# Where the last output-projection unit is split, and which expert loads take the freed places

## The chip, the cores and the metric

The kernel runs on one core of a Trainium2 chip. The core has a matrix engine (TensorE, PE in the profile), a vector engine (VectorE, DVE), a scalar engine (ScalarE, ACT), GpSimd (POOL) and SyncE (SP), which here issues nearly all DMA transfers. They work from an on-chip memory, SBUF, and matrix products land in the banks of PSUM. Engines wait for one another through semaphores. The metric is the time of one execution in microseconds.

## The reference

Two transformer blocks run one after the other on 256 tokens of 1024 channels. The first is a gated mix of three branches and a feed-forward part. The second has two kinds of attention, an output projection, and a mixture of 32 experts, of which each token uses two:

```python
mixed = concat(rmsnorm(o_dil), rmsnorm(o_sb))
x = x + gate_mix * (mixed @ w_out)
h2 = modulate(rmsnorm(x, g_ffn), shift_ffn, scale_ffn)
y = hierarchical_moe(h2, w_group, w_expert, w_gate, w_up, w_down)
x = x + gate_ffn * y
return rmsnorm(x, g_final)
```

The change lies between `mixed @ w_out` and the first expert. The norm ahead of the experts needs the sum of squares of every token over its 1024 channels, and the routing needs the product of `x` with `w_group` and `w_expert` (36 columns, the logits), scaled by that norm.

## The kernel before

**Units.** All weights but those of the experts come as a stream of units of 1 MiB. A unit lands in a raw buffer. ScalarE copies each half of it, rounded, to a high part (`sph`, line 1314), and GpSimd subtracts that from the raw data and writes the low part (`spl`, line 2596). TensorE then makes three products for each pair of operands (lines 538 to 540). High and low part of a unit together fill one of `NSP` = 3 split places, `u.n % NSP`. ScalarE may write a half of a unit only when TensorE has used the unit three before it (`half_used`, line 1313). The output projection is the last stage of the stream, with the four units `w_out_units` 0 to 3. Units 0 and 3 therefore share a split place, and units 1 and 2 have the two others.

**TensorE's order around the change.** `out_part(n, ks, ...)` multiplies unit n, in two halves of 128 output channels each. After the attention it runs: unit 0 (its last 12 matmuls in each half), unit 1, unit 2, then `logits(0)` to `logits(3)`, then the whole of unit 3 (48 matmuls), then `logits(4)` to `logits(6)`, the first matmuls of the sums of squares (line 1114), `logits(7)`, and the last matmuls of the sums (line 1118). The transposes of line 1127 follow. `logits(k)` (line 1096, 4 matmuls) waits for channel block k of the new `x`, `XTN[:, k]`.

**VectorE.** For k = 0 to 7 it makes `XTN[:, k]` out of PSUM (line 2353), as soon as half k of the eight halves is used. From k = 2 on it first waits for the square k - 1 and adds it to the running sum `SQA` (line 2350). Behind these come the reciprocal root and the routing, from line 2363.

**ScalarE.** After the attention's last parts it takes the splits of the remaining units, the last of which is unit 3, and then makes the eight squares (line 1774), in program order. The root of the sums is line 1776.

**Expert loads.** The weights of the 32 experts (6 MiB each) come as half loads of 1 MiB, numbered 0, 1, 2, ... in `EXPERT_WEIGHTS`; from 34 on most are taken in pairs of 2 MiB. Each goes to a place in a ring of SBUF regions. The early loads go to regions that other data leaves free one after the other, and the list `ISSUED` gives the order in which SyncE issues them. SyncE waits before each for what frees its place, and everything behind it in the list waits too. Loads 15 to 22 go to what the output projection frees: 15 and 16 to `ring5`, 17 and 18 to `ring6`, 19 and 20 to `ring7` (the split places of the units 1, 2 and 3 by `TOP_OF`), 21 and 22 to `ring8` (the projection's left operand). Load 14 goes to the raw buffer of the last unit, once that is split. Loads from 24 on wait until an expert has used the earlier load in their place; load 24 waits for the first quarter of expert 0.

Of the kernel before, what the change touches and what calls it, by code (L numbers as in the profile page):

```python
# [22 lines left out]
NSP = 3  # L23
# [78 lines left out]
def k8(t):  # L102
    return t.rearrange("p (k n) -> p k n", k=8)
# [119 lines left out]
def program(nc, I, out, const_at):  # L223
    with ExitStack() as ctx:
# [43 lines left out]
            return v if k is None else v.rearrange("p (k n) -> p k n", k=k)  # L268

        units, first, ada_at, ff_at, wide_at, conv_at = stream_plan()  # L270


        G = ar(0, 6144).rearrange("p (i t n) -> p i t n", i=3, t=2)
# [52 lines left out]
        w_out_units = [units[first["w_out_2"] + n] for n in range(4)]  # L326
        RING = [at(f"ring{n}", TOP - 4096 - 4096 * n, 4096) for n in range(2)]
        RING += [at("ring2", O_RAW, 4096), at("ring3", O_XB, 4096), at("ring4", O_RAW + 4096, 4096)]
        TOP_OF = {n + 4: O_SPL + 4096 * (w_out_units[n].n % NSP) for n in (1, 2, 3)}
        for n in (5, 6, 7):  # L330
            RING.append(at(f"ring{n}", TOP_OF[n], 4096))
        RING += [at("ring8", O_XA, 4096), at("ring9", O_AR + 10496, 4096)]
# [5 lines left out]
        SLOT += [ar(6144, 2048), ar(8192, 2048)]  # L338

        FIRST = [0, 1, 2, NS, 3, 4, 5, NS + 1, 6, 7, 8, 9, NS - 2] + list(range(10, NS - 2)) + [NS - 1]  # L340
        ISSUED = [0, 1, 2, 4, 8, 12, 5, 6, 9, 10, 11, 3, 7, 13, 15, 16, 14] + list(range(17, 23)) + list(range(24, 34))
        ISSUED += [23] + list(range(34, len(EXPERT_WEIGHTS)))

        def place(s):
# [158 lines left out]
        def tensor(e):  # L503
# [42 lines left out]
            def fm_unit(v, name, xT, ready):  # L546

                u = units[v]
                H, L = k8(SPH[u.n % NSP]), k8(SPLO[u.n % NSP])
                b = bank(name)  # L550
                claim(b)
                for h in range(2):
                    c = slice(h * 128, h * 128 + 128)
                    w.wait_ge(lo_ok, 2 * u.n + h + 1)
                    for k in range(8):
                        if ready:
                            w.wait_ge(*ready(k))
                        mm = product(ps[b][:, h * 256:h * 256 + 256], H[:, k, c], L[:, k, c], xT[0][:, k, :],
                                     xT[1][:, k, :], k == 0, k == 7)
                    mm.then_inc(w.up(half_used), 1)  # L560
                return b

            def tm_part(stage, n, outs, xT, ready, tiles, done):

                u, i = units[unit_at(stage, n)], n % 2
                H, L = k4(SPH[u.n % NSP]), k4(SPLO[u.n % NSP])
                for h in range(2):
                    w.wait_ge(lo_ok, 2 * u.n + h + 1)
                    for tt in tiles:
                        c = slice(tt * 128, tt * 128 + 128)  # L570
                        for k in (2 * h, 2 * h + 1):
                            if ready:
                                w.wait_ge(*ready(4 * i + k, tt))
                            mm = product(outs[tt], xT[0][:, 4 * i + k, c], xT[1][:, 4 * i + k, c], H[:, k, :], L[:, k, :],
                                         i == 0 and k == 0, i == 1 and k == 3)
                        if tt == 0 and i == 1 and h == 1:
                            mm.then_inc(w.up(tile0_mm), 1)
                    if done:
                        mm.then_inc(w.up(half_used), 1)
# [37 lines left out]
            def wide(v, bb, xT, start, stop, tiles=(0, 1)):  # L617

                u = units[v]
                H, L = k2(SPH[u.n % NSP]), k2(SPLO[u.n % NSP])  # L620
                for k in range(2):
                    w.wait_ge(lo_ok, 2 * u.n + k + 1)
                    for j in range(2 * tiles[0], 2 * tiles[-1] + 2):
                        cc, cn = slice((j // 2) * 128, (j // 2) * 128 + 128), slice((j % 2) * 512, (j % 2) * 512 + 512)
                        claim(bb[j])
                        mm = product(ps[bb[j]][:, :], xT[0][:, k, cc], xT[1][:, k, cc], H[:, k, cn], L[:, k, cn],
                                     start and k == 0, stop and k == 1)
                        if stop and k == 1 and j < 3:
                            mm.then_inc(w.up(wide_mm), 1)
                    if 1 in tiles:  # L630
                        mm.then_inc(w.up(half_used), 1)
# [379 lines left out]
            def out_part(n, ks, start, stop, halves=(0, 1)):  # L1011

                u = units[first["w_out_2"] + n]
                H, L = k8(SPH[u.n % NSP]), k8(SPLO[u.n % NSP])
                for h in halves:
                    if start:
                        b = bank(("w_out_2", 2 * n + h))
                        claim(b)
                        held.add(b)
                    b = bank_of["w_out_2", 2 * n + h]  # L1020
                    c = slice(h * 128, h * 128 + 128)
                    w.wait_ge(lo_ok, 2 * u.n + h + 1)
                    for k in ks:
                        w.wait_ge(act_lo, part_at["heads_s" if k >= 4 else "heads_d"] + k % 4 // 2 + 1)
                        mm = product(ps[b][:, 0:256], H[:, k, c], L[:, k, c], XA[0][:, k, :], XA[1][:, k, :],
                                     start and k == ks[0], stop and k == ks[-1])
                    if stop:
                        mm.then_inc(w.up(half_used), 1)
                        free[b] = [(x_ok, X4 + 2 * n + h + 1)]
# [72 lines left out]
                logits(k)  # L1102
            release(0)
            out_part(3, range(8), True, True)
            for k in range(4, 7):
                logits(k)
            for n in (1, 2, 3):
                release(n)
            b = bank("ss")
# [2 lines left out]
            w.wait_ge(sqa_ok, 6)  # L1112
            for tt in range(2):
                e.matmul(ps[b][:, tt:tt + 1], SQA[:, tt * 128:tt * 128 + 128], ones[:, 0:1], start=(tt == 0), stop=False)
            logits(7).then_inc(w.up(rt_mm), 1)
            w.wait_ge(hs_ok, 8)
            for tt in range(2):
                mm = e.matmul(ps[b][:, tt:tt + 1], SQ2[1][:, tt * 128:tt * 128 + 128], ones[:, 0:1], start=False, stop=(tt == 1))
            mm.then_inc(w.up(ss_mm), 1)
            free[b] = [(rs_ok, 1)]  # L1120
            for i in range(4):
                tt, half = i % 2, i // 2
# [171 lines left out]
        def scalar(e):  # L1294
# [9 lines left out]
            def split_one(between=None):  # L1304
# [4 lines left out]
                for h in range(2):  # L1309
                    if h and between:  # L1310
                        between()
                    if u.n >= NSP:
                        w.wait_ge(half_used, 2 * (u.n - NSP) + (h + 1 if u.same else 2))
                    e.activation(u.half(SPH[u.n % NSP], h), u.half(RAW[u.slot], h), ACTF.Copy).then_inc(w.up(hi_ok), 1)  # L1314

            def take(v):

# [1268 lines left out]
        def gpsimd(e):  # L2586
# [3 lines left out]
            def split_one():  # L2590
# [2 lines left out]
                begun[0] += 1  # L2593
                for h in range(2):
                    w.wait_ge(hi_ok, 2 * u.n + h + 1)
                    e.tensor_tensor(u.half(SPLO[u.n % NSP], h), u.half(RAW[u.slot], h), u.half(SPH[u.n % NSP], h),  # L2596
                                    ALU.subtract).then_inc(w.up(lo_ok), 1)

            split_one()
# [7 lines left out]
        def sync(e):  # L2607
# [38 lines left out]
            for n, s in enumerate(ISSUED):  # L2646
# [25 lines left out]
                elif s in (6, 7, 11):  # L2672
                    pass
                elif 15 <= s < 23:
                    w.wait_ge(half_used, 2 * w_out_units[min((s - 13) // 2, 3)].n + 2)
                elif s == 23:
                    w.wait_ge(y0_mm, 1)
                else:
# [180 lines left out]
```

## Time and profile before

| | us |
|---|---|
| median of 3 runs | 1093.62 |
| lowest and highest | 1093.51, 1094.03 |
| profiled execution, time | 1094.04 |
| profiled execution, span of the trace | 1092.3 |
| TensorE busy | 996.4 |
| VectorE, ScalarE, GpSimd busy | 529.8, 391.5, 498.3 |
| mean DMA rate over the span | 313 GB/s |

The profile has a page (busy time of the engines, 40 slices of the span, the chain of work that ended last) and a trace that can be asked for windows, for the instructions of an engine in order of time, and for the DMA issues with their time to landing. Times in the trace count from the start of the span. A row of a timeline gives start, duration, engine, line, operation, tiles and shapes, how many instructions are merged into it, and in brackets how long the engine had been idle and what ended that.

### The profile page before, as it was taken

How to read it: one execution, taken by the hardware profiler on the slowest of the kernel's cores; microseconds unless marked ns; L12 is line 12 of the kernel's file. 1: busy time of each engine (PE TensorE's matmuls, PEld its weight loads, DVE VectorE, ACT ScalarE, POOL GpSimd, SP SyncE). 2: the span in 40 equal slices, each digit the busy share in tenths (PEclk: the TensorE clock that was granted, in tenths of full speed). 3: DMA queues.
4: the chain of work that ended last, by engine and by line, in shares of the span. 5: the costliest groups of instructions: out<-in, count | busy, mean ns of one | idle time of the engine just before them, and what ended most of it. 6: DMA issues, size and time to landing. Idle time of an engine off the chain costs nothing.

```text
span 1092.3 us, 16613 instructions
## 1 busy us (share of the span) xinstructions
PE 996.4 (91%) x6890; PEld 733.6 (67%) x6890; DVE 529.8 (49%) x984; ACT 391.5 (36%) x558; POOL 498.3 (46%) x210
## 2 busy tenths in 40 slices
PE   7999999999999999999899999999968687878786
PEld 6989988788788888887898895544434343434332
DVE  1998896665367776214358543323222121222224
ACT  7345555554475444556597441000000000000002
POOL 6987699879598887987666510000000000000000
PEclk9999999999999999999899999999999899999888
DMA  9745455547469999638343989999999999999995
GB/s 381 280 168 180 153 194 193 182 186 278 154 248 397 356 360 377 245 116 338 131 155 116 367 347 417 429 424 428 424 428 426 426 428 425 427 427 426 427 422 239
DMA packets 38527, 341.96 MB, mean 313 GB/s; under 512 B 4273, under 2 KB 4657, under 8 KB 6322
## 3 DMA queue, kind: packets, MB, share of 16 engines
q1 hardware_dynamic: 37152, 337.82, 77.2%
q10 hardware_dynamic: 1298, 3.05, 0.8%
q8 instruction: 55, 0.90, 0.3%
q14 instruction: 22, 0.18, 0.0%
HBM read 339.81 MB, written 1.05 MB: 312 GB/s over the span
## 4 chain that ended last, share of the span: by engine, by line
PE 63%; DMA 24%; DVE 6%; ACT 3%; SPq 1%; issue 1%; POOL 0%; another core or an unknown queue 0%; DVEq 0%; ACTq 0%
DMA ring<-in_gu 17%; PE ps L538 15%; PE ps L540 15%; PE ps L539 15%; DMA ring<-in_dn 7%; PE ps L1187 5%; PE ps L1229 4%; PE ps L1218 2%; PE ps L1168 1%; SPq L2680 1%; PE ps L720 1%; ACT sph L1314 1%; DVE ar L2294 1%; SPq L2654 0%; PE ps L1206 0%
## 5 line engine op out<-in xcount | busy, mean ns | idle before, releaser
L2596 POOL TENSOR_TENSOR spl<-raw,sph 128x1024 fp32r<-128x1024 f32 x204 | 496.3, 2467 | 139.9 <-ACT sph L1314 139.8
L1314 ACT ACTIVATE sph<-raw 128x1024 fp32r<-128x1024 f32 x204 | 208.4, 1056 | 107.6 <-PE ps L540 93.3
L2604 POOL TENSOR_SCALAR ring<-ring,SM 128x512 f32<-128x512 f32 x1 | 1.6, 1567 | 449.9 <-DVE SM L1854 449.9
L1806 ACT ACTIVATE ar<-ps 64x256 f32<-64x256 f32 x32 | 12.1, 377 | 331.8 <-PE ps L1187 331.8
L538 PE MATMUL ps<-sph,xbh 128*128 128x512 f32 x304 | 119.6, 394 | 0.4 <-DVE ar L2261 0.4
L540 PE MATMUL ps<-sph,xbl 128*128 128x512 f32 x304 | 118.5, 390 | 0.0
L539 PE MATMUL ps<-spl,xbh 128*128 128x512 f32 x304 | 118.4, 389 | 0.0
L1229 PE MATMUL ps<-ar,ar 128*128 128x512 f32 x240 | 111.9, 609 | 0.0
L538 PE MATMUL ps<-xah,sph 128*128 128x256 f32 x320 | 92.1, 288 | 1.1 <-DVE xal L1869 0.8
L1899 DVE SCALAR_TENSOR_TENSOR ps<-ar,COL,ps 128x256 f32<-128x256 f32 x232 | 92.1, 480 | 0.0
L539 PE MATMUL ps<-xal,sph 128*128 128x256 f32 x320 | 90.5, 283 | 0.0
L540 PE MATMUL ps<-xah,spl 128*128 128x256 f32 x320 | 90.5, 283 | 0.0
L1187 PE MATMUL ps<-ring,ar 128*32 128x256 f32 x944 | 63.7, 413 | 25.9 <-DMA ring<-in_gu 25.9
L2538 DVE TENSOR_TENSOR ar<-ar,ps 64x256 f32<-64x256 f32 x32 | 13.5, 423 | 141.3 <-ACT ar L1806 141.3
L1229 PEld LDWEIGHTS ps<-ar,ar 128*128 128x128 f32 x240 | 45.6, 201 | 47.6 <-issue 47.6
L538 PE MATMUL ps<-sph,xah 128*128 128x512 f32 x192 | 75.7, 394 | 1.5 <-POOL spl L2596 1.5
L539 PE MATMUL ps<-spl,xah 128*128 128x512 f32 x192 | 74.8, 389 | 0.0
L540 PE MATMUL ps<-sph,xal 128*128 128x512 f32 x192 | 74.8, 389 | 0.0
L1187 PEld LDWEIGHTS ps<-ring,ar 128*32 128x32 f32 x944 | 31.2, 115 | 63.2 <-issue 47.9
L1187 PE MATMUL ps<-ring,xg 128*32 128x256 f32 x912 | 58.6, 398 | 15.3 <-DMA ring<-in_gu 14.7
L1218 PE MATMUL ps<-ring,ar 128*32 128x512 f32 x464 | 55.9, 595 | 17.3 <-DMA ring<-in_dn 16.1
L538 PEld LDWEIGHTS ps<-sph,xbh 128*128 128x128 f32 x304 | 57.1, 188 | 12.3 <-DVE ar L2261 0.8
(332 smaller groups left out, 1708.2 us busy)
## 6 DMA issues: line engine op xcount, KB each, us to landing
raw<-in_stream SPq DMA_DIRECT2D x127, 1024.0 KB, 5.8
ring<-in_gu SPq DMA_DIRECT2D x46, 2048.0 KB, 45.6
ring<-in_dn SPq DMA_DIRECT2D x22, 2048.0 KB, 45.7
ring<-in_gu SPq DMA_DIRECT2D x24, 1024.0 KB, 9.5
ring<-in_dn SPq DMA_DIRECT2D x14, 1024.0 KB, 10.9
ar<-in_gu SPq DMA_DIRECT2D x7, 1024.0 KB, 30.7
slotx<-in_gu SPq DMA_DIRECT2D x5, 1024.0 KB, 43.8
ar<-in_dn SPq DMA_DIRECT2D x3, 1024.0 KB, 47.8
```

The source lines that it names most:

```text
L538: e.matmul(o, sh, mh, start=start, stop=False)
L539: e.matmul(o, sh, ml, start=False, stop=False)
L540: return e.matmul(o, sl, mh, start=False, stop=stop)
L720: mm = e.matmul(ps[b][:, d * 256:d * 256 + 256], WP[:, g, k, d * 128:d * 128 + 128], ZP[:, 2 * g + k, 16:272], start=(k == 0), stop=(k == 1))
L1187: mm = e.matmul(ps[b][32 * q:32 * q + 32, 0:256], XG[g % 2][:, k, (x % 4) * 32:(x % 4) * 32 + 32], W[:, q // 2, k % 2, (q % 2) * 256:(q % ...
L1218: mm = e.matmul(ps[b][32 * j:32 * j + 32, :], HE[x % 2][:, 32 * j:32 * j + 32], W[:, 2 * (j % 2) + j // 2, :], start=True, stop=True)
L1229: mm = e.matmul(ps[yb[tt * 2 + nn]][:, :], SWT[x % 2][:, tt * 128:tt * 128 + 128], YP[x % 2][:, nn * 512:nn * 512 + 512], start=False, sto ...
L1314: e.activation(u.half(SPH[u.n % NSP], h), u.half(RAW[u.slot], h), ACTF.Copy).then_inc(w.up(hi_ok), 1)
L1806: e.activation(HS[x % 2][0:64, :], ps[bank_of["gu", x]][0:64, 0:256], ACTF.Silu).then_inc(w.up(hsa_ok), 1)
L1899: e.scalar_tensor_tensor(out=acc if k < 30 else CVO[:, c, :], in0=CV[:, c, k:k + 256], scalar=tap(k, c), in1=acc, op0=ALU.mult, op1=ALU.add)\
L2538: e.tensor_tensor(h[0:64, :], h[0:64, :], ps[bank_of["gu", x]][64:128, 0:256], ALU.mult).then_inc(w.up(hsm_ok), 1)
L2596: e.tensor_tensor(u.half(SPLO[u.n % NSP], h), u.half(RAW[u.slot], h), u.half(SPH[u.n % NSP], h), ALU.subtract).then_inc(w.up(lo_ok), 1)
```

## The change

Unit 3 is split into the place of unit 1 in place of that of unit 0 (`split_at`), so ScalarE waits for the halves of unit 1 before it writes them. The split place of unit 0 becomes `ring5`, and that of unit 1, now also unit 3's, becomes `ring7`. So loads 15 and 16 wait for unit 0, 17 and 18 for unit 2, and 19 to 22 for unit 3. Load 14 is issued behind 17 and 18. On TensorE, the first matmuls of the sums of squares come straight behind unit 3, then `logits(4)` and `logits(5)`, then the last matmuls of the sums, then `logits(6)` and `logits(7)`.

```diff
+        last_unit = units[first["w_out_2"] + 3]
+
+        def split_at(u):
+
+            return (u.n + 1 if u is last_unit else u.n) % NSP
...
-        TOP_OF = {n + 4: O_SPL + 4096 * (w_out_units[n].n % NSP) for n in (1, 2, 3)}
+        TOP_OF = {ring: O_SPL + 4096 * split_at(w_out_units[n]) for ring, n in ((5, 0), (6, 2), (7, 3))}
...
-        ISSUED = [0, 1, 2, 4, 8, 12, 5, 6, 9, 10, 11, 3, 7, 13, 15, 16, 14] + list(range(17, 23)) + list(range(24, 34))
+        ISSUED = [0, 1, 2, 4, 8, 12, 5, 6, 9, 10, 11, 3, 7, 13, 15, 16, 17, 18, 14] + list(range(19, 23)) + list(range(24, 34))
...
             release(0)
             out_part(3, range(8), True, True)
-            for k in range(4, 7):
-                logits(k)
             for n in (1, 2, 3):
                 release(n)
             b = bank("ss")
...
             w.wait_ge(sqa_ok, 6)
             for tt in range(2):
                 e.matmul(ps[b][:, tt:tt + 1], SQA[:, tt * 128:tt * 128 + 128], ones[:, 0:1], start=(tt == 0), stop=False)
-            logits(7).then_inc(w.up(rt_mm), 1)
+            for k in (4, 5):
+                logits(k)
             w.wait_ge(hs_ok, 8)
             for tt in range(2):
                 mm = e.matmul(ps[b][:, tt:tt + 1], SQ2[1][:, tt * 128:tt * 128 + 128], ones[:, 0:1], start=False, stop=(tt == 1))
             mm.then_inc(w.up(ss_mm), 1)
+            logits(6)
+            logits(7).then_inc(w.up(rt_mm), 1)
...
-                    if u.n >= NSP:
+                    if u is last_unit:
+                        w.wait_ge(half_used, 2 * w_out_units[1].n + h + 1)
+                    elif u.n >= NSP:
                         w.wait_ge(half_used, 2 * (u.n - NSP) + (h + 1 if u.same else 2))
-                    e.activation(u.half(SPH[u.n % NSP], h), u.half(RAW[u.slot], h), ACTF.Copy).then_inc(w.up(hi_ok), 1)
+                    e.activation(u.half(SPH[split_at(u)], h), u.half(RAW[u.slot], h), ACTF.Copy).then_inc(w.up(hi_ok), 1)
...
                 elif 15 <= s < 23:
-                    w.wait_ge(half_used, 2 * w_out_units[min((s - 13) // 2, 3)].n + 2)
+                    w.wait_ge(half_used, 2 * w_out_units[(0, 2, 3, 3)[(s - 15) // 2]].n + 2)
```

## Rows read from the trace of the kernel before

**Rows 1.** The page's 40 slices of the span: GB/s that the DMA engines moved.

```profile
GB/s 381 280 168 180 153 194 193 182 186 278 154 248 397 356 360 377 245 116 338 131 155 116 367 347 417 429 424 428 424 428 426 426 428 425 427 427 426 427 422 239
```

**Rows 2.** Windows: length, busy PE, PEld, DVE, ACT, POOL, PEclk, DMA share, GB/s.

```profile
633.00:636.00 3.00, 3.00 (x28) 3.00 (x27) 1.49 (x3) 1.30 (x4) 3.00 (x2) 1.00 0.00 0
637.00:1040.00 403.00, 338.19 (x3082) 176.24 (x3082) 112.85 (x266) 32.00 (x78) 0.00 (x0) 0.96 1.01 425
...
652.00:656.00 4.00, 3.89 (x34) 3.63 (x38) 1.87 (x7) 2.15 (x5) 0.00 (x0) 1.00 1.02 424
```

**Rows 3.** The chain that ended last, 1040 to 1092: its last transfer (start, us).

```profile
1048.62 31.83 DMA ring<-in_dn
```

**Rows 4.** Timeline of SyncE: issues of loads 15, 17, 19 and 24.

```profile
635.09 0.33 SPq L2680 DMA_DIRECT2D ring<-in_dn  x1
...
637.97 0.33 SPq L2680 DMA_DIRECT2D ring<-in_gu  x1
...
645.51 0.33 SPq L2680 DMA_DIRECT2D ring<-in_gu  x1
...
657.00 0.33 SPq L2680 DMA_DIRECT2D ring<-in_gu  x1
```

**Rows 5.** Issue to landing: issued 605.29 to 608.73 (min), 635.09, 645.51, 657.00.

```profile
DMA to landing us min/median/max: 5.2/6.7/7.3
...
DMA to landing us min/median/max: 5.1/5.1/5.1
...
DMA to landing us min/median/max: 8.1/8.1/8.1
...
DMA to landing us min/median/max: 6.6/6.6/6.6
```

**Rows 6.** The page's DMA issues: count, KB each, median us from issue to landing.

```profile
ring<-in_gu SPq DMA_DIRECT2D x46, 2048.0 KB, 45.6
```

**Rows 7.** Timeline of TensorE: logits 0 to 3, unit 3's first matmul, what follows.

```profile
637.77 1.87 PE L1096 MATMUL ps<-cst,xtn 128*128 128x36 f32 x16
639.48 0.36 PE L538 MATMUL ps<-xah,sph 128*128 128x256 f32 x1
...
645.32 1.43 PE L1096 MATMUL ps<-cst,xtn 128*128 128x36 f32 x12
...
647.47 0.58 PE L1118 MATMUL ps<-cst,ar 128*128 128x1 f32 x4
...
652.02 0.38 PE L1151 MATMUL ps<-AS,cst 128*128 128x32 f32 x2 [1.27 <-DVE AS L2402]
```

**Rows 8.** Timeline of VectorE: blocks of XTN (L2353), adds (L2350), first routing step.

```profile
630.78 0.48 DVE L2353 SCALAR_TENSOR_TENSOR xtn<-ps,SM,ar 128x256 f32<-128x256 f32 x1 [1.25 <-PE ps L540]
...
633.92 0.73 DVE L2350 TENSOR_TENSOR ar<-ar,ar 128x256 f32<-128x256 f32 x1 [1.22 <-ACT ar L1774]
634.76 0.48 DVE L2353 SCALAR_TENSOR_TENSOR xtn<-ps,SM,ar 128x256 f32<-128x256 f32 x1
635.73 1.48 DVE L2350 TENSOR_TENSOR ar<-ar,ar 128x256 f32<-128x256 f32 x1 [0.48 <-ACT ar L1774]
...
638.27 0.42 DVE L2350 TENSOR_TENSOR ar<-ar,ar 128x256 f32<-128x256 f32 x1 [0.48 <-ACT ar L1774]
...
648.66 0.54 DVE L2363 SCALAR_TENSOR_TENSOR RT<-ps,SM 128x36 f32<-128x36 f32 x2
```

**Rows 9.** Timeline of ScalarE: unit 3's first half, first two squares, the root.

```profile
630.83 1.06 ACT L1314 ACTIVATE sph<-raw 128x1024 fp32r<-128x1024 f32 x1 [2.27 <-PE ps L540]
...
633.18 0.70 ACT L1774 ACTIVATE ar<-xtn 128x256 f32<-128x256 f32 x2
...
648.09 0.26 ACT L1776 ACTIVATE SM<-ps,cst 128x2 f32<-128x2 f32 x1 [1.64 <-PE ps L1118]
```

**Rows 10.** Timeline of GpSimd: the two halves of the last unit.

```profile
631.97 2.40 POOL L2596 TENSOR_TENSOR spl<-raw,sph 128x1024 fp32r<-128x1024 f32 x1 [9.73 <-ACT sph L1314]
...
634.33 2.59 POOL L2596 TENSOR_TENSOR spl<-raw,sph 128x1024 fp32r<-128x1024 f32 x1
```

More of the change, by code:

```diff
@@ L548, in fm_unit @@
                 u = units[v]
-                H, L = k8(SPH[u.n % NSP]), k8(SPLO[u.n % NSP])
+                H, L = k8(SPH[split_at(u)]), k8(SPLO[split_at(u)])
                 b = bank(name)
@@ L565, in tm_part @@
                 u, i = units[unit_at(stage, n)], n % 2
-                H, L = k4(SPH[u.n % NSP]), k4(SPLO[u.n % NSP])
+                H, L = k4(SPH[split_at(u)]), k4(SPLO[split_at(u)])
                 for h in range(2):
@@ L619, in wide @@
                 u = units[v]
-                H, L = k2(SPH[u.n % NSP]), k2(SPLO[u.n % NSP])
+                H, L = k2(SPH[split_at(u)]), k2(SPLO[split_at(u)])
                 for k in range(2):
@@ L1013, in out_part @@
                 u = units[first["w_out_2"] + n]
-                H, L = k8(SPH[u.n % NSP]), k8(SPLO[u.n % NSP])
+                H, L = k8(SPH[split_at(u)]), k8(SPLO[split_at(u)])
                 for h in halves:
@@ L2595, in split_one @@
                     w.wait_ge(hi_ok, 2 * u.n + h + 1)
-                    e.tensor_tensor(u.half(SPLO[u.n % NSP], h), u.half(RAW[u.slot], h), u.half(SPH[u.n % NSP], h),
+                    e.tensor_tensor(u.half(SPLO[split_at(u)], h), u.half(RAW[u.slot], h), u.half(SPH[split_at(u)], h),
                                     ALU.subtract).then_inc(w.up(lo_ok), 1)
```

## The prediction

> **What bounds the kernel now.** I read the page's 40 slices first. In the GB/s row [rows 1] the last 14 slices before the final one stand at 422 to 429: whatever TensorE does there, the 16 DMA engines are full. The table of windows [rows 2] makes this sharp. From 637 to 1040 us the DMA share is 1.01 at 425 GB/s, so a load of 1 MiB (1.049 MB) takes 1.049/425 = 2.47 us of the stream. Just ahead of that stretch there is a hole: 633 to 636 stands at 0.00. Then the chain of what ended last [rows 3]: its late pieces are transfers, and the last expert load lands at 1048.62 + 31.83 = 1080.45, with 12 us of the last expert's work and the output behind it. So the end is the end of the load stream plus a fixed tail, and a change pays only by what it moves the stream.
>
> The stream waits for places. The issues of SyncE [rows 4] show what ends the hole: load 15 at 635.09, when the second output unit is used up. Each later issue then meets some backlog. A load issued into idle DMA engines lands after 5.1 us, and 5.2 in the other such case; the one issued at 645.51 lands after 8.1, the one at 657.00 after 6.6 [rows 5]. The excess over 5.1 is the backlog at that moment: 8.1 - 5.1 = 3.0 us and 6.6 - 5.1 = 1.5 us. **The second number decides this case**: it belongs to expert load 24, the first that has to wait for an expert to be computed (gu_mm, the first quarter of expert 0). In the median the loads of the stream land 45.6 us behind their issue [rows 6], so nothing later is as tight. If the stream is moved ahead by more than 1.5 us and the routing in front of expert 0 isn't, a new hole opens there.
>
> **Part 1: loads 15 and 16 into the first unit's place.** Times of TensorE: between 639.48 and 645.32 the last unit's 48 matmuls start, 0.12 us apart [rows 7]. A half unit of 12 is 1.44 us. VectorE takes the first half of unit 0 at 630.78 [rows 8], so the halves of units 0 and 1 end at 630.78, 632.22, 633.66 and 635.10; the last agrees with the issue at 635.09 [rows 4]. Load 15 goes out at 632.2 in place of 635.1: 2.9 us earlier. It lands at 632.2 + 5.1 = 637.3, load 16 at 639.7. Load 17 still waits for unit 2, at 637.97 [rows 4], and can't land before 637.97 + 5.1 = 643.1, while the stream alone would give 639.7 + 2.5 = 642.2: 0.9 us are lost again. So after this stop the stream is 2.9 - 0.9 = 2.0 us ahead. Moving load 14 behind 17 and 18 costs nothing: its wait (the last unit's low parts) ends before load 19 may go.
>
> **Part 2: the last unit split into the second unit's place.** ScalarE's two halves, the first at 630.83 with 1.06 us [rows 9], waited for unit 0 and began 0.06 behind its halves. Now they wait for the halves of unit 1: start 633.72, end 634.78, and start 635.16, end 636.22. TensorE doesn't feel that directly: GpSimd's first half then runs from 634.86 to 637.26 (2.40 [rows 10]), the second to about 639.8, and TensorE wants them at 639.5 and 642.4. What is queued behind the wait does. On ScalarE the eight squares of the sums stand behind the split in program order. The first two ran at 633.18 (0.70 for both [rows 9]); now they start at 636.13 and end at 636.83. VectorE may not make xtn 2 until it has added square 1 (it waits hs_ok, adds, then goes on), so that add comes at 636.86.
>
> And the adds run into GpSimd. The add L2350 takes 0.42 alone, as at 638.27 [rows 8]. The one at 633.92 took 0.73 and ended 634.65, 0.28 after GpSimd's first half ended (631.97 + 2.40 = 634.37 [rows 10]); the one at 635.73 took 1.48 and ended 637.21, again 0.28 after GpSimd's second half (634.33 + 2.59 = 636.92). So an add (two operands in SBUF) is held until the running subtraction ends, while L2353 (one operand in PSUM) took its usual 0.48 at 634.76, inside it. Now: the add at 636.86 is held to 637.26 + 0.28 = 637.54. From an add's end to the next block of xtn it is 0.10, the block takes 0.48, and from there to the next add, with a square between, it is 0.49 (635.24 to 635.73) [rows 8]. So xtn 2 runs from 637.64 to 638.12 and the next add is ready at 638.61. GpSimd's second half is running: with the 2.59 that it took before it ends at 637.22 + 2.59 = 639.81, and the add at 640.09. xtn 3 runs from 640.19 to 640.67. TensorE needs xtn 3 for logits(3), which stands ahead of the last unit in its queue. Before, xtn 3 was ready at 637.21 + 0.10 + 0.48 = 637.79, well before its turn (16 matmuls from 637.77 on, 0.11 apart, the last four from 639.05 [rows 7]). Now logits(3) starts at about 640.67 + 0.15 = 640.82 (for the release I take a little over the 0.10 that VectorE needs for its own) and the last unit 0.45 later, at 641.27 in place of 639.48. **The last unit is 1.8 us late**, and with it the places that it frees.
>
> **Part 3: sums of squares ahead of the last logits.** Before, behind the last unit came 12 logits matmuls, 4 for the sums, 4 for logits(7) and 4 for the rest of the sums, which ended at 647.47 + 0.58 = 648.05 [rows 7]; then the root at 648.09 [rows 9], a reciprocal, and L2363 at 648.66 [rows 8], 0.61 behind the sums. From 645.32 to 647.47 20 matmuls start, so one takes 0.1075. With the new order, and the last unit ending 1.8 later (647.11), the last four for the sums start 12 matmuls on, at 648.40, and end at 648.98; the root's way would let L2363 start at 649.59. But it needs logits(6) and logits(7) too, which now stand last: the 24th matmul starts at 647.11 + 23 x 0.1075 = 649.58 and ends 0.28 later, and L2363 comes at about 649.95. Against 648.66 that is 1.3 late: of the 1.8 the new order gives 0.5 back. Without the delay, part 3 would be worth that 0.5 and no more, since 24 matmuls have to run in either order.
>
> **The sum.** Load 19 goes out at 645.51 + 1.8 = 647.3 and lands at 652.4 (the stream alone would give 650.4); four loads end at 652.4 + 3 x 2.47 = 659.8 against 661.0 before: 1.2 ahead. Load 24 goes out at 657.00 + 1.3 = 658.3 and lands at 658.3 + 5.1 = 663.4 against 657.00 + 6.6 = 663.6: **0.2 us ahead**. In general the gain is the least of 2.0, 3.0 - d and 1.5 - (d - 0.5), with d the delay of the last unit; for d = 1.8 the three are 2.0, 1.2 and 0.2. Later issues have more backlog than that and the stream is full to 1080, so this is what reaches the end. The profiled execution has a span of 1092.3 and a time of 1094.04; changed, it would have 1092.1 and 1093.8. It lies 0.42 above the median of the runs, so against the median the forecast is 1093.62 - 0.2 = 1093.4. The landing into idle engines (5.1 or 5.2 [rows 5]) moves it by 0.1, the release of logits(3) (nothing to 0.3) by 0.15, and where exactly the held adds end by about 0.3: 1092.9 to 1094.0 for this case alone.
>
> The landing is also priced by the Trainium skill ("SBUF — State Buffer", The DMA setup-cost knee): 2 us and the bytes at 436 GB/s, an estimate of 4.4 us for 1 MiB. By that the backlog at load 24 would be 2.2 and the gain 0.9 us, 1092.7; the trace shows 5.1 and I go by it.
>
> **Rivals.**
> (B) The adds aren't held as before, because GpSimd and VectorE fall otherwise in time. Then the add at 636.86 ends at 637.29, xtn 2 at 637.88, xtn 3 at 639.37, logits(3) from 639.52, the last unit at 639.97: d = 0.5. Gain: 1.5 - 0.0 = 1.5, so 1092.1. Against it: both adds that met a subtraction were held [rows 8, 10].
> (C) Slower than before: the add at 636.86 misses the gap between GpSimd's two halves. It is ready only 0.4 us before the first half ends (637.26), and the second half is queued already. If ScalarE's squares come 0.4 later, or GpSimd wins, it is held to 639.66 + 0.28 = 639.94; xtn 2 ends 640.53, xtn 3 at 642.03, the last unit starts at 642.6: d = 3.1. Load 24 goes out 2.6 late: 1.5 - 2.6 = -1.1, 1094.7. It decides from a lateness of 0.4 us. For it: the margin; against it: at 634.37 the add won that gap with the second half waiting [rows 8, 10]. The Trainium skill ("SBUF — State Buffer", Who interferes with whom) says that of a VectorE instruction with two SBUF inputs and a GpSimd one the first to issue gets the shared port pair for the whole instruction and the other fully blocks; by this rule this change, which puts the adds behind the split, costs what C or the forecast says, and the two held adds of the trace agree.
> (D) The stall never reaches the stream: the delay of the last unit is near nothing, or first bytes come sooner when a load follows closely. Then the gain is the 2.0 of part 1, at most 2.2: 1091.5. For it: the hole is real [rows 2] and the change does reach into it. Against it: the first squares ran straight behind the split [rows 9], and the program's order leaves them no way round it.
> (E) TensorE's clock falls behind the new idle stretch of 1.6 us (639.2 to 640.8) and the last unit runs at 1.2 GHz in place of 2.4: 5.8 us more, about 1099. Against it: the idle of 1.27 ahead of 652.02 [rows 7] left the granted clock at 1.00 from 652 to 656 [rows 2].
>
> **How the numbers follow.** Forecast 0.55, B 0.13, C 0.14, D 0.15, E 0.03. The range from 1091.5 (D) to 1094.8 (C) leaves out E, the far half of D and the tails of C, under 2 in 10. About 0.2% (2.2 us) is what a measurement can tell from no change: 1091.4 to 1095.8. Faster by more needs the far end of D: 0.06. Slower by more needs E or twice C: 0.04. Within: 0.90.
>
> **What would show it.** Right: an issue at 632.2 and the DMA engines at work again 2.9 us sooner; ScalarE's first squares at 636.1 in place of 633.2; two held adds that end 0.28 behind GpSimd; TensorE idle ahead of logits(3) for 1.6 us; the last unit from about 641.3; L2363 near 650.0; small holes ahead of loads 19 and 24, the latter landing within 0.3 of 663.5. Wrong: logits(3) at 639.1 without idle (then D), one short add of 0.42 at 638.6 (B), an add of about 3 us (C), or a landing in idle engines well off 5.1.

## The result and the profile after

The changed kernel takes **1096.45 us** in the median (1094.64 to 1097.69) against 1093.7 for the kernel before, timed beside it (1092.99 to 1094.92). The ratio is 1.0022, 95% interval 1.0015 to 1.0028: slower by 1.6 to 3.1 us. I had forecast 1093.4 with 1094.8 as the upper end, so the direction and the range were both wrong. The 15 times of the changed kernel lie in two groups, five from 1094.64 to 1095.15 and ten from 1096.28 to 1097.69, with none between; what parts them isn't known.

The profiled execution took 1096.87 us and belongs to the upper group. Up to load 13, the last one issued ahead of load 15, it does the same as before, 0.62 us later by its own clock; that is taken off wherever I write "in the clock of before" (for each other kernel likewise, by its issue of load 13). The 0.62 is no part of the change. All line numbers are a few higher (L1096 is L1101, L2353 is L2361). The page's GB/s row and the last transfer of the chain, to be held against [rows 1, 3]:

```profile
GB/s 380 279 168 179 155 192 192 188 186 281 142 258 397 356 363 371 240 111 339 128 151 118 378 347 388 429 425 427 424 428 427 425 427 426 428 426 426 426 423 235
...
1052.25 31.03 DMA ring<-in_dn
```

From the 26th slice on the stream is as full as it was. The last expert load lands at 1052.25 + 31.03 = 1083.28, or 1082.66 in the clock of before, against 1080.45: 2.2 us later. So the loss was made ahead of that stretch, in the stream, as the bound says. Windows of after, with the columns of [rows 2]:

```profile
633.00:636.00 3.00, 3.00 (x28) 3.00 (x27) 0.31 (x1) 1.36 (x2) 0.54 (x1) 1.00 0.73 205
...
646.00:650.00 4.00, 4.00 (x38) 4.00 (x36) 1.07 (x3) 0.85 (x3) 0.00 (x0) 1.00 0.79 252
650.00:654.00 4.00, 4.00 (x24) 4.00 (x24) 3.05 (x18) 2.43 (x4) 0.00 (x0) 0.57 0.95 395
654.00:658.00 4.00, 3.91 (x36) 3.75 (x35) 1.28 (x6) 3.39 (x6) 0.00 (x0) 1.00 1.01 424
658.00:662.00 4.00, 4.00 (x52) 2.95 (x50) 3.41 (x14) 0.00 (x0) 0.00 (x0) 1.00 0.82 274
662.00:670.00 8.00, 7.45 (x94) 3.72 (x97) 1.83 (x5) 3.08 (x7) 0.00 (x0) 1.00 1.00 375
670.00:1040.00 370.00, 307.68 (x2778) 151.77 (x2774) 98.34 (x213) 21.13 (x56) 0.00 (x0) 0.95 1.01 426
```

The last two columns carry it. The hole at 633 to 636 is partly filled (205 GB/s where there was 0), but three new dips stand behind it: 252, 274 and 375. They are the starts of loads 19, 24 and 26. The same windows of before:

```profile
646.00:650.00 4.00, 4.00 (x38) 4.00 (x38) 1.34 (x8) 2.04 (x5) 0.00 (x0) 1.00 1.01 426
...
658.00:662.00 4.00, 3.45 (x48) 2.63 (x51) 1.62 (x7) 1.50 (x4) 0.00 (x0) 1.00 0.99 403
662.00:670.00 8.00, 7.00 (x88) 3.26 (x80) 1.99 (x5) 1.95 (x4) 0.00 (x0) 1.00 1.00 412
```

SyncE's issues of loads 15, 19, 24 and 26 and what each took to land:

```profile
632.82 0.33 SPq L2688 DMA_DIRECT2D ring<-in_dn  x1
DMA to landing us min/median/max: 7.4/7.4/7.4
...
647.79 0.33 SPq L2688 DMA_DIRECT2D ring<-in_gu  x1
DMA to landing us min/median/max: 7.5/7.5/7.5
...
659.43 0.33 SPq L2688 DMA_DIRECT2D ring<-in_gu  x1
DMA to landing us min/median/max: 5.8/5.8/5.8
...
663.89 0.33 SPq L2688 DMA_DIRECT2D ring<-in_dn  x1
DMA to landing us min/median/max: 7.6/7.6/7.6
```

In the clock of before: 632.2, 647.2, 658.8 and 663.3. The stall came as predicted; GpSimd, VectorE, ScalarE and TensorE (start, us; what ended the idle time):

```profile
635.46 4.90 POOL L2604 TENSOR_TENSOR spl<-raw,sph 128x1024 fp32r<-128x1024 f32 x2 [12.60 <-ACT sph L1322]
```

```profile
637.41 0.73 DVE L2358 TENSOR_TENSOR ar<-ar,ar 128x256 f32<-128x256 f32 x1 [4.10 <-ACT ar L1782]
...
639.21 1.43 DVE L2358 TENSOR_TENSOR ar<-ar,ar 128x256 f32<-128x256 f32 x1 [0.48 <-ACT ar L1782]
640.75 0.48 DVE L2361 SCALAR_TENSOR_TENSOR xtn<-ps,SM,ar 128x256 f32<-128x256 f32 x1
...
650.40 0.55 DVE L2371 SCALAR_TENSOR_TENSOR RT<-ps,SM 128x36 f32<-128x36 f32 x2 [0.46 <-PE ps L1101]
```

```profile
634.32 1.06 ACT L1322 ACTIVATE sph<-raw 128x1024 fp32r<-128x1024 f32 x1 [5.14 <-PE ps L545]
635.70 1.06 ACT L1322 ACTIVATE sph<-raw 128x1024 fp32r<-128x1024 f32 x1 [0.32 <-PE ps L545]
636.67 0.71 ACT L1782 ACTIVATE ar<-xtn 128x256 f32<-128x256 f32 x2
```

```profile
641.29 0.63 PE L1101 MATMUL ps<-cst,xtn 128*128 128x36 f32 x4 [1.48 <-DVE xtn L2361]
641.76 0.36 PE L543 MATMUL ps<-xah,sph 128*128 128x256 f32 x1
...
650.19 3.40 PE L1133 MATMUL ps<-cst,xtn 128*128 128x128 f32 x16
653.39 1.30 PE L1149 MATMUL ps<-cst,xtn 128*128 128x128 f32 x8
654.53 0.31 PE L1157 MATMUL ps<-AS,cst 128*128 128x32 f32 x2
```

The two adds are held (0.73 and 1.43 us in place of 0.42), TensorE waits 1.48 us ahead of logits(3), the last unit starts 641.76 - 0.62 - 639.48 = 1.66 us later, and routing starts at 649.78 in the clock of before, 1.1 later. What I had not counted is the pace of the 16 transposes L1133: 3.40 us, most of them 0.213 us apart. In before they took 1.94, 0.109 apart:

```profile
647.91 1.94 PE L1127 MATMUL ps<-cst,xtn 128*128 128x128 f32 x16
```

The windows there:

```profile
650.00:651.00 1.00, 1.00 (x9) 1.00 (x9) 0.53 (x3) 0.00 (x0) 0.00 (x0) 0.74 0.88 369
651.00:652.00 1.00, 1.00 (x7) 1.00 (x6) 0.83 (x6) 0.76 (x2) 0.00 (x0) 0.50 0.95 401
...
653.00:654.00 1.00, 1.00 (x7) 1.00 (x6) 0.86 (x6) 0.83 (x2) 0.00 (x0) 0.55 0.96 393
654.00:655.00 1.00, 1.00 (x12) 1.00 (x11) 0.02 (x1) 0.98 (x2) 0.00 (x0) 1.00 1.06 442
```

The granted clock is 0.50 (1.2 GHz, of two levels the lower) for 3.4 us behind the stall and a run of small matmuls; before has 1.00 in its window with the transposes (646 to 650 above).

### The profile page after: what moved, and what is told of

Read it like the earlier page. It is cut to its first block, busy times and chain, and to the rows that moved or that the text cites. A ratio compares the mean times of both kernels' runs of the same rounds, so it can differ in the third digit from the quotient of the medians.

```text
span 1095.1 us, 16614 instructions
## 1 busy us (share of the span) xinstructions
PE 999.3 (91%) x6890; PEld 736.5 (67%) x6890; DVE 529.8 (48%) x984; ACT 391.9 (36%) x558; POOL 498.3 (46%) x210
## 4 chain that ended last, share of the span: by engine, by line
PE 63%; DMA 25%; DVE 6%; ACT 3%; SPq 1%; issue 1%; POOL 0%; DVEq 0%; ACTq 0%
DMA ring<-in_gu 17%; PE ps L543 15%; PE ps L545 15%; PE ps L544 15%; PE ps L1193 5%; DMA slotx<-in_gu 4%; PE ps L1235 4%; DMA ring<-in_dn 3%; PE ps L1224 2%; PE ps L1174 1%; SPq L2688 1%; ACT sph L1322 1%; PE ps L725 1%; DVE ar L2302 1%; PE ps L1212 1%
## 6 DMA issues: line engine op xcount, KB each, us to landing
ring<-in_dn SPq DMA_DIRECT2D x22, 2048.0 KB, 45.6
```

## The experiments

Three theories run through the expectations: the loss comes from the last unit's delay alone (stall), from loads issued shortly ahead of their turn (start-up), or from TensorE's clock (clock). "Mean landing" is worked out from the trace: each load has 16 completions, one for each DMA engine, and the landing that the profile prints is the last. A load's turn is the moment at which the DMA engines, the first of them in the table below, are done with the load ahead. All kernels stand in the clock of before. The times of before beside them were 1093.78 (first batch), 1093.8 (second), 1094.22 (third) and 1093.59 (fourth).

**1. Part 3 alone.** The kernel before with only the diff of the logits and sums: logits 4 and 5 behind the first sums, 6 and 7 behind the last.

> The kernel before, with part 3 alone: the sums of squares ahead of the last logits, no other place for the last unit and no other load order. Stall theory (the loss comes from the last unit's delay behind logits(3), part 3 is harmless): L2363 comes 0.5 us sooner than in the kernel before, load 24 is issued 0.5 sooner and the time is 1093.2 to 1093.7, ratio 0.9995 to 1.000. Start-up theory (a load that is issued shortly ahead of its turn pays a start-up on the DMA engines of about a microsecond): load 24 keeps its lead, so the same. Sums theory (the new order itself costs, by a fall of TensorE's clock in the stretch of small matmuls): 1094.5 or more, with a granted clock below 1.00 between 645 and 655 us.

```diff
-            for k in range(4, 7):
-                logits(k)
...
-            logits(7).then_inc(w.up(rt_mm), 1)
+            for k in (4, 5):
+                logits(k)
...
+            logits(6)
+            logits(7).then_inc(w.up(rt_mm), 1)
```

1093.56, ratio 0.9998 [0.9989, 1.0007]; load 24 is issued 0.5 us sooner and lands where it did, because the stream sets its turn. The 0.5 us is real in this execution, and by itself worth nothing; the sums theory (1094.5 or more) falls.

**2. Part 3 undone**, the rest of the change kept.

```diff
             out_part(3, range(8), True, True)
+            for k in range(4, 7):
+                logits(k)
...
-            for k in (4, 5):
-                logits(k)
+            logits(7).then_inc(w.up(rt_mm), 1)
...
-            logits(6)
-            logits(7).then_inc(w.up(rt_mm), 1)
```

> The changed kernel with part 3 undone (old order of logits and sums behind the last unit), split place and loads as changed. Stall theory: 0.5 us later routing than the changed kernel, time 1096.5 to 1097.5. Sums theory: back to 1094 or less. Start-up theory: as the changed kernel, 1096 to 1097.5.

1096.97, ratio 1.0027 [1.0017, 1.0037], as the stall and the start-up theory both said. Load 24 is issued at 660.3, 1.5 later than in after. Here the clock fell twice, the first time right behind the stall, so the 1.5 is not part 3 alone.

**3. The early loads undone**: the split stays in the second unit's place, the two loads wait for unit 1 again.

```diff
-                    w.wait_ge(half_used, 2 * w_out_units[(0, 2, 3, 3)[(s - 15) // 2]].n + 2)
+                    w.wait_ge(half_used, 2 * w_out_units[(1, 2, 3, 3)[(s - 15) // 2]].n + 2)
```

> The changed kernel with loads 15 and 16 held until the second unit is used, as before (their place is free earlier, but they wait); the last unit still splits into the second unit's place. The split's cost is then alone. Stall theory: the last unit is 1.7 us late, the stream isn't ahead, load 19 has 1.3 us of its backlog of 3.0 left and load 24 none: 1093.8 to 1095.5. Start-up theory: the stream is idle as long as before ahead of load 15 and runs dry at loads 19 and 24 as in the changed kernel, so no better than 0.5 us from the changed kernel: 1096 to 1097.5, which would say that the early loads bring nothing.

1096.63, ratio 1.0026 [1.0015, 1.0037]: **without the early loads the rest of the change, above all the split, costs as much as the whole.** That misses the stall theory's 1093.8 to 1095.5 and lies in the start-up theory's 1096 to 1097.5. The profiled execution, the fastest of its eight (1095.7), isn't a clean match for that of after, though: the clock is at 0.50 twice, once more than there, the first time under the last unit, and loads 19 and 24 go out 1.4 us later than in after. Its windows (columns of [rows 2]):

```profile
639.00:643.00 4.00, 3.76 (x20) 3.77 (x21) 2.34 (x6) 1.25 (x3) 0.00 (x0) 0.60 1.01 426
...
651.00:652.00 1.00, 1.00 (x6) 1.00 (x6) 0.85 (x5) 0.81 (x2) 0.00 (x0) 0.50 1.02 426
```

**4. logits(3) behind the last unit**, so that the held adds don't stop the unit.

```diff
-            for k in range(4):
+            for k in range(3):
                 logits(k)
...
-            for k in (4, 5):
+            for k in (3, 4, 5):
                 logits(k)
```

> The changed kernel with logits(3) moved behind the last unit, so that TensorE doesn't wait for the held adds. The last unit starts near 639.0, no idle stretch ahead of it. Stall theory: load 19 is issued near 645.1, load 24 near 656.5, the stream is 2.0 us ahead and the time is 1091.5 to 1092.3, ratio 0.998 to 0.999. Start-up theory: load 24 and its neighbours are issued with no lead, each pays a start-up, and the time is no better than the kernel before, 1093.5 to 1095.5. Clock theory (the idle stretch of 1.5 us drops TensorE's clock later on): granted clock 1.00 throughout 640 to 656.

1096.35, ratio 1.0017 [1.0008, 1.0026]. The unit was in time (load 19 issued at 645.0), but TensorE then stood still for 1.17 us ahead of the sums, which wait for the same late adds, and the clock fell under the transposes (at 649.9): load 24 went out at 658.5. The stall was moved, not removed, so the miss of the stall theory's 1091.5 to 1092.3 decides nothing here.

**5. The squares ahead of the split** on ScalarE: squares 0 and 1, the unit's first half, square 2, the second half, the rest.

```diff
-            for n in range(1, 4):
-                take(first["w_out_2"] + n)
-            for k in range(8):
+            def square(k):
...
+            square(0)
+            square(1)
+            split_one(lambda: square(2))
+            for k in range(3, 8):
+                square(k)
```

> The changed kernel with ScalarE's order mended: squares 0 and 1 ahead of the last unit's split, square 2 between its halves. So xtn 3 is ready before its turn and TensorE doesn't stand ahead of logits(3); everything else as changed. Stall theory (the lateness of the last unit alone makes the loss, the stream is one server with a start-up of 5.1 us): the last unit starts at 639.4 or sooner (times of the kernel before), load 19 goes out at 645.5, load 24 at 656.5, the time is 1091.6 to 1092.6. Clock theory (part of the loss is TensorE at 1.2 GHz for 3 to 4 us between 640 and 655, brought on by the idle stretch together with the small matmuls behind the last unit): no such stretch in the profile, and runs that lie together like those of sums_alone; the same time as the stall theory. Start-up theory (a load that is issued less than about 2 to 3 us ahead of its turn waits longer than in an idle engine): loads 17, 19 and 24 each lose about a microsecond, the time is 1093 to 1094.5.

1094.03, ratio 1.0006 [0.9997, 1.0015]. VectorE of this kernel:

```profile
633.80 2.43 DVE L2362 TENSOR_TENSOR ar<-ar,ar 128x256 f32<-128x256 f32 x1 [0.92 <-ACT ar L1779]
636.34 0.48 DVE L2365 SCALAR_TENSOR_TENSOR xtn<-ps,SM,ar 128x256 f32<-128x256 f32 x1
```

An add is still held, for 2.43 us, but there is only one ahead of the fourth block of xtn, which ends at 636.82, or 638.1 in the clock of before; TensorE wants it at 639.05 [rows 7] and feels nothing. Load 19 is issued at 645.5 as before. Against the 1096.45 of the change this is 2.4 us less, 1.7 by the ratios: the stall with what it brings. The stall theory wanted 1091.6 to 1092.6 and falls; the start-up theory's 1093 to 1094.5 holds the time. This execution has one fall of the clock (at 648.2), and load 24 goes out at 657.1.

**6. The same without the early loads** (the edit of 3).

> As squares_first, but loads 15 and 16 wait for the second unit, as in the kernel before: what is left of the change is then the sums' order, the split place and load 14 behind 17 and 18. Stall and clock theory: as sums_alone, 1093.2 to 1093.9, and squares_first is 1.5 to 2.0 us faster than this one. Start-up theory: squares_first and this one within 0.5 us of each other, both near the kernel before.

1094.17, ratio 1.0005 [0.9995, 1.0014]: with no stall to pay for, the early loads bring nothing that shows, where the stall and clock theories wanted 1.5 to 2.0 us.

**7. The stall kept, its idle time filled** with 12 matmuls whose results are never used, ahead of logits(3).

```diff
-            for k in range(4):
+            for k in range(3):
                 logits(k)
+            for _ in range(12):
+                e.matmul(ps[rb[0]][:, 256:512], XA[1][:, 0, 0:128], XA[0][:, 0, :], start=False, stop=False)
+            logits(3)
```

> The changed kernel with 12 matmuls of 256 columns between logits(2) and logits(3), on operands that lie ready, into columns of a PSUM bank that nobody reads: TensorE is busy where it stood idle, and logits(3) comes no later. Clock theory, idle stretch as its cause: the granted clock stays at 1.00 from 634 to 660, load 24 goes out 0.7 us sooner than in the changed kernel, 1094.0 to 1095.5, few runs above 1096. If the small matmuls behind the last unit bring the clock down: as the changed kernel, 1096 to 1097, with the stretch at 0.50 behind them. Stall theory: as the changed kernel.

1094.72, ratio 1.0013 [1.0004, 1.0022]. Load 19 goes out at 647.2 as in after; the clock doesn't fall in the profiled execution, and load 24 goes out at 658.14 against 658.80. So the fall costs 0.66 us at load 24. That the filling kept the fall away isn't shown: by experiments 10 and 11 below it is partly chance. The medians of the two differ by 1.7, but their intervals overlap, and the profiled mean landing of the last load differs by only 0.4, so I don't claim more than 0.7 for it. This profiled execution is one of the two slowest of its eleven (1096.38), with no fall there, so a slow time doesn't need the fall. In it 12.55 us pass from the last landing to the end, where after and before have 11.82; the tail isn't quite fixed.

**8. The logits spread**: experiment 5 with logits 4 and 5 between the last unit's halves and 6 ahead of the last sums.

```diff
-            out_part(3, range(8), True, True)
+            out_part(3, range(8), True, True, (0,))
+            for k in (4, 5):
+                logits(k)
+            out_part(3, range(8), True, True, (1,))
```

> As squares_first, with logits(4) and logits(5) between the halves of the last unit and logits(6) ahead of the last sums: the run of small matmuls behind the last unit is 16 in place of 24, and the last unit ends 0.9 us later. Clock theory, small matmuls as its cause: clock at 1.00 there, no upper group of runs (none above 1095), and at least as fast as squares_first; load 19 goes out 0.9 later, L2363 as in squares_first. Stall theory: load 19 is the tighter one now, 0.5 us slower than squares_first.

1093.61, ratio 0.9999 [0.999, 1.0009]. No fall of the clock, load 19 issued at 646.4, 24 at 656.9. The stall theory's half a microsecond more than experiment 5 isn't there.

**9. The same without the early loads.**

> spread (the squares ahead of the last unit's split, logits 4 and 5 between that unit's halves, logits 6 ahead of the last sums) without its early loads: loads 15 and 16 wait for unit 1 as in the kernel before. Spread came out level with before, 2.0 us ahead in its stream at load 18 and 0.5 behind at load 26. If the early loads bring nothing because the lead is lost at loads 19, 24 and 26, this comes out the same or up to 0.5 sooner: 1093.1 to 1093.7. If the early loads did bring something that another cost ate, it comes out later than spread, 1094.5 or more.

1093.67, ratio 0.9992 [0.9983, 1.0001]. Level with before and with 8; the best ratio of all, though its interval holds 1. Windows of 8 and then of 9 (last column GB/s):

```profile
655.00:658.00 3.00, 3.00 (x43) 2.07 (x43) 2.47 (x12) 0.00 (x0) 0.00 (x0) 1.00 1.01 363
...
661.00:664.00 3.00, 3.00 (x43) 1.51 (x36) 0.85 (x2) 0.38 (x1) 0.00 (x0) 1.00 1.00 330
```

```profile
655.00:658.00 3.00, 3.00 (x43) 1.95 (x43) 2.33 (x9) 0.00 (x0) 0.00 (x0) 1.00 1.03 431
...
661.00:664.00 3.00, 3.00 (x60) 1.63 (x52) 0.85 (x2) 0.87 (x3) 0.00 (x0) 1.00 1.01 415
```

With early loads the DMA share is near 1 and the rate low: packets lie in the engines for longer where a new load begins (at load 26 up to 1.6 us, against 1.0 in 9; the median of both is 0.31). After the fifth load behind the hole the stream was 2.0 us ahead of that of before; at load 19 it lost 0.9 of that, and the two dips shown took the rest and 0.5 more.

**10 and 11. Load 26 held on SyncE**, in the kernel of experiment 1, first by ten and by twenty-five waits on a semaphore reached long ago:

```diff
+                if s == 26:
+                    for _ in range(10):
+                        e.wait_ge(dv_mm, 2)
```

> The kernel before with part 3 alone (sums_alone, which ran at the time of before), and load 26, the first of expert 0's down weights' successors, held on SyncE by ten waits on a semaphore that has long been reached. Nothing else changes and no load is early. In sums_alone load 26 is issued 3.3 us before the first DMA engine is done with load 25, and the stream loses nothing there; in the kernels with early loads that distance is 2.3 to 2.5 us and the stream loses 0.8 to 1.0 us. Theory 'distance' (a load whose issue comes too short before its turn costs the stream time though no DMA engine has run out of packets): if the ten waits take 0.8 us or more, the distance is 2.5 us or less and the stream loses 0.8 us or so at load 26, time 1094.3; if they take 0.4 us, the distance is 2.9 and nothing is lost, 1093.6. Rival 'early' (the loss at load 26 comes from something the early loads leave behind, such as DMA engines spread apart): nothing is lost, 1093.6.

> As held26_10, with twenty-five such waits ahead of load 26. Theory 'distance': if they take 1 to 1.5 us, the distance falls to 1.8 to 2.3 us and the stream loses 0.8 to 1.3 us, time 1094.4 to 1094.9. Rival 'early': the first DMA engine could go on at issue plus the 2.3 us or so of an idle start, so at most 0.3 us is lost, time 1093.6 to 1093.9.

1094.19 and 1093.73, ratios 1.0001 [0.9992, 1.001] and 0.9997 [0.9988, 1.0006]. The waits took no time (load 26 is issued 4.5 us after load 24, as in experiment 1), so neither theory was tested. One thing they do show: no instruction but SyncE's differs from experiment 1, and yet the profiled executions of both have a fall of the clock at 648.0, and that of experiment 1 has none. The fall is partly chance. Its price shows here too: load 24 is issued at 657.1 with the fall and at 656.45 without.

**12 and 13. Load 26 held by real events**: ScalarE's Silu of expert 0, and VectorE's product behind it.

```diff
+                if s == 26:
+                    w.wait_ge(hsa_ok, 1)
```

> sums_alone (level with before, no early load) with load 26 held on SyncE until expert 0's Silu (ScalarE, ended 1.3 us after load 26 was issued in sums_alone). The ten and twenty-five waits of held26_10 and held26_25 took no time, so those two say nothing of the distance; this one waits for a real event. The distance from load 26's issue to the first DMA engine being done with load 25 falls from 3.3 us to 2.0 us. Theory 'distance': the mean landing of load 26 slips by 0.8 to 1.0 us against the last one plus 2.5 us, as in the kernels with early loads, and the time is 1094.2 to 1094.6. Rival 'early' (the loss at load 26 needs the early loads): issue plus the 4.6 us that an idle start takes is 666.8 in the clock of before, under the 667.3 at which the unheld load lands in the mean: nothing is lost, 1093.6.

> As held26_hs, held until VectorE's product behind the Silu (1.8 us after the issue in sums_alone): the distance is 1.5 us. Theory 'distance': 1.0 to 1.3 us lost at load 26, time 1094.4 to 1094.9. Rival 'early': issue plus 4.6 us is 667.3, at which it lands anyway: 0 to 0.1 us lost, 1093.6 to 1093.7.

1093.89 and 1093.85, ratios 1.0002 [0.9992, 1.0012] and 1.0003 [0.9994, 1.0013]. Their issue and landing, hs and then hm:

```profile
662.46 0.33 SPq L2683 DMA_DIRECT2D ring<-in_dn  x1
DMA to landing us min/median/max: 5.7/5.7/5.7
```

```profile
661.33 0.33 SPq L2683 DMA_DIRECT2D ring<-in_dn  x1
DMA to landing us min/median/max: 7.9/7.9/7.9
```

Worked out from the traces, in the clock of before. "dist" is the first engine's completion of the load ahead less this issue; "lost" is the mean landing less (that of the load ahead + 2.475):

```
kernel           load  issue   dist   mean landing   lost
before           15    635.1  -3.2    issue + 4.6    (idle engines)
before           19    645.5   3.8    issue + 6.7    0.1
before           24    657.0   2.3    issue + 5.3    0.1
before           26    661.5   2.8    issue + 6.0    0.2
late_loads       19    648.6   0.7    issue + 4.7    1.2
late_loads       24    660.2   0.1    issue + 4.7    1.6
late_loads       26    664.7   2.5    issue + 5.5    0.2
held26_hs        26    662.9   1.2    issue + 5.0    0.6
held26_hm        26    663.4   0.9    issue + 5.0    1.0
spread           19    646.4   0.9    issue + 4.7    1.0
spread           24    656.9   1.2    issue + 5.0    0.8
spread           26    661.4   2.6    issue + 6.6    1.0
squares_first    26    661.6   2.3    issue + 6.5    0.9
after            19    647.2   0.1    issue + 4.9    1.8
after            24    658.8   0.2    issue + 4.7    1.4
after            26    663.3   2.4    issue + 6.2    0.9
```

What the holds tell: a load issued close to its turn lands, in the mean, 4.7 to 5.0 us after its issue, and the stream loses just what that is later than its own pace. The distance theory as I wrote it (a loss with engines still full) wants 0.8 us at a distance near 2 to 2.5; load 24 of before at 2.3 and that of squares_first_late at 2.0 lose 0.1, so distance alone doesn't make the loss. In the chip time the holds' 0.4 and 0.9 us (mean landing of the last load 1077.66 and 1078.17 against 1077.26) don't clear the interval: 1093.89 and 1093.85 decide between no two of the times expected.

Late_loads tells one thing more. Its load 26 loses only 0.2, but load 27 right behind it loses 0.7. Loads 26 and 27 together lose 0.6 to 1.1 us in seven kernels: the six with early loads and late_loads, which has none. What the seven share is a load 24 issued 1.2 us or less ahead of its turn. Around load 26 their longest packets are 1.4 to 2.0 us. In the six others without a hold load 24 has 2.0 to 2.7 us, the two loads lose 0.1 to 0.25, and the longest packets are 0.9 to 1.0. So the early loads aren't needed for this loss. The same shows at load 19 of logits3_behind: 2.1 us ahead of its turn it loses 1.1, and load 17, the last one to start the stream anew, was issued 1.1 ahead of its turn.

## Why the prediction was wrong, step by step

- **What bounds the kernel: right.** The mean landing at load 26 is 1.97 us later than before and that of the last load 1.95 later: what is lost by load 26 stays to the end. The rest of the 2.2 at the last landing is the spread among the 16 engines.
- **Part 1: the issue right, the worth wrong.** Load 15 at 632.2 as said, its mean landing 2.6 sooner, and after the fifth load of the stretch the stream was 1.8 ahead in the mean (2.0 in spread), as worked out. Only its last engine wasn't: it took 7.4 us, not 5.1.
- **Part 2: right and well sized.** Squares at 636.05 in the clock of before (predicted 636.13), idle 1.48 (1.6), d = 1.66 (1.8), both adds held.
- **Part 3: right.** 1.1 late at L2371 (1.3); alone it gives load 24 0.5 us.
- **The sum: here it failed, at the term 1.5 - (d - 0.5).** I took the backlog at load 24 as 6.6 - 5.1 [rows 5], from the landings printed, which are those of the last DMA engine. A few late engines (the last at 663.5 against a mean of 662.3) made before look well supplied. In the mean the load landed 5.3 us after issue where a start needs 4.7 to 5.0: the margin was 0.3 to 0.6, not 1.5. Load 19's was 6.7 - 4.7 = 2.0, not 3.0. With those, and my own issue at 658.3, load 24 lands 0.7 to 1.0 us *later* than before instead of 0.2 sooner. So the early loads by themselves could never bring more than 0.3 to 0.6, whatever they filled, since load 24 was nearly bound by its issue already (with the 0.5 us of part 3, 0.8 to 1.1). In experiments 5 and 8, without the stall, load 24 did land 0.2 and 0.35 us sooner than in before, in the mean, and load 26 took more than that back. And every part of a microsecond by which routing comes later than that is paid in full.
- **E: the mechanism right, place and price wrong.** I had the clock fall under the last unit, for 5.8 us. It fell behind it, for 3.4 us under the transposes, and cost 0.66 at load 24 (experiment 7). Under the last unit it did fall in experiments 2 and 3. The idle of 1.27 us with no fall [rows 7, 2], my evidence against, was no good evidence: a fall comes in one execution and not in the next.
- **Load 26: not foreseen, and its cause open.** I wrote that nothing later is as tight, from a median of 45.6 us. But [rows 6] are the loads of 2 MiB; 24 to 33 are of 1 MiB, and load 26 of before reads

```profile
661.46 0.33 SPq L2680 DMA_DIRECT2D ring<-in_dn  x1
...
DMA to landing us min/median/max: 7.1/7.1/7.1
```

In the mean it is 6.0, a margin of 1.0 to 1.3. In all six kernels with early loads the stream lost 0.6 to 1.0 us at its start, though the load was issued 2.1 to 2.6 us ahead of its turn. In late_loads it lost 0.9 at loads 26 and 27 together. The loss goes with a load 24 issued too close to its turn, with early loads or without; what carries it on to load 26, these runs don't show.
- **The account of after**, in mean landing: load 24 is 1.25 later than before (0.7 from its predicted issue of 658.3 with a start of 4.7, 0.5 from the later issue, which is the clock's fall), load 26 adds 0.9 - 0.2 = 0.7: 1.95. The first two terms are accounted for; the third is measured, not explained.
- **B, C, D.** B and C are refuted by the rows: the adds were held, and the first won the gap. D's 1091.5 is refuted by experiments 5 and 8: without any stall the early loads gave 1094.03 and 1093.61.
- The rule of the Trainium skill ("SBUF — State Buffer", Who interferes with whom) held at the four adds of before and after: each ended 0.28 us behind GpSimd's end. The setup-cost estimate of the Trainium skill (same page, The DMA setup-cost knee), 4.4 us for 1 MiB, lies nearer to the mean landing in idle engines (4.6) than to the printed 5.1 that I preferred; for the pace of a stream the mean is what counts, but at 4.4 the forecast would have erred further.

## What to carry to other kernels

Filling a hole in a load stream is worth no more than the smallest margin that any later load has between its issue and its turn; look for that one first, and read it from the mean over the DMA engines, since the printed landing is the slowest engine's. Work placed behind a wait on an in-order queue is moved with the wait: here the eight small squares stood behind one split, and that cost more than the loads could give. When one part of a change frees time that nothing uses (part 3), it only pays where it shortens what issues the tightest load.

## What the hardware showed that I had not expected

- The 16 DMA engines drift apart. Load 15 issued into nearly idle engines (distance -0.2) landed 7.43 us after issue in after, while the mean was 4.91; in before, into engines idle for 3 us, 5.06 and 4.63. In squares_first load 19 landed 9.49 after issue, its mean 5.54.
- Of the profiled executions, five show no fall of TensorE's clock between 600 and 760 us (before, experiments 1, 7, 8 and 9) and ten show one or two, each of about 3.4 us at 0.50, near 641 or 648 to 655. In six of the ten TensorE had no idle stretch over 0.15 us between 630 and 656 (experiments 5, 6 and 10 to 13).
- Ten or twenty-five waits on a semaphore that has long been reached took SyncE no time that the trace shows, behind a wait that had to be waited for.
